# A hybrid mixer layer with 32 experts: expert weights through a ring of eight buffers, operands of the token sort stored chunk by chunk, the sort split 128 and 384

## The reference

```
h = rmsnorm(x, norm1_g)
u = h @ w_in                                   # 2048 x 5632
x = x + concat(short_conv(u_a), attention(u_q, u_k, u_v), conformer_conv(u_c)) @ w_out
h = rmsnorm(x, norm2_g)
grp = argmax(softmax(h @ rg_w + rg_b))         # 4 groups of 8 experts
e1, e2 = top 2 of softmax(h @ re_w + re_b) inside the group
for each expert e of 32, for the tokens that chose it:
    y[token] += gate * ((silu(h @ w_gate[e]) * (h @ w_up[e])) @ w_down[e])
out = rmsnorm(x + y, final_g)
```

## Time and profile before

| | us |
|---|---|
| median of 3 runs | 1378.87 (1377.28 to 1378.97) |
| the profiled execution, its own time | 1379.87 |
| its span, first to last instruction | 1378.1 |
| TensorE matmul busy | 1243.5 (90%) |
| TensorE weight load busy | 701.5 (51%) |
| VectorE busy | 508.7 (37%) |
| ScalarE busy | 276.9 (20%) |
| DMA moved | 471.69 MB, mean 342 GB/s |

### The profile page before, as it was taken

One profiled execution on the slowest core, in us unless ns is written; L12 is line 12 of the kernel. 1 busy time (PEld: TensorE's weight loads), 2 busy tenths in 40 slices (PEclk: granted clock), 3 DMA queues, 4 the chain that ended last, 5 costly groups with the idle time before them and its releaser, 6 DMA issues.

```text
span 1378.1 us, 16838 instructions
## 1 busy us (share of the span) xinstructions
PE 1243.5 (90%) x6468; PEld 701.5 (51%) x6468; DVE 508.7 (37%) x906; ACT 276.9 (20%) x383; POOL 6.0 (0%) x27
## 2 busy tenths in 40 slices
PE   5999999989989998989898989898988888988996
PEld 5999999978877433333333333333333333333332
DVE  5365968655444422222222232222222222222224
ACT  5433444445332100010000010000110000100002
POOL 1000000000000000000000000000000000000000
PEclk9999999999989999999999999999999999999998
DMA  8555454538466699999999999999999999999993
GB/s 274 196 184 184 150 185 148 169 141 296 162 244 244 259 428 428 428 430 428 428 428 429 428 428 430 428 428 431 427 428 430 428 428 430 428 427 430 429 423 148
DMA packets 63580, 471.69 MB, mean 342 GB/s; under 512 B 5911, under 2 KB 6423, under 8 KB 37692
## 3 DMA queue, kind: packets, MB, share of 16 engines
q1 hardware_dynamic: 63548, 471.24, 83.6%
HBM read 469.13 MB, written 2.10 MB: 342 GB/s over the span
## 4 chain that ended last, share of the span: by engine, by line
PE 50%; DMA 45%; DVE 2%; issue 2%; SPq 1%; ACT 1%; DVEq 0%; ACTq 0%
DMA ring<-in_w_up 44%; PE bank L1275 23%; PE bank L1442 17%; PE bank L1419 2%; PE bank L1491 2%; PE bank L1443 1%; PE bank L1504 1%; SPq L384 1%; DMA stage<-in_w_in 1%; PE bank L1385 1%; DVE x_tok L1148 0%; ACT w_hi L341 0%; DVE zone_u L833 0%; PE bank L1352 0%; DVE x_tok L1236 0%
## 5 line engine op out<-in xcount | busy, mean ns | idle before, releaser
L1442 PE MATMUL bank<-ring,win 128*64 128x512 f32 x976 | 431.9, 595 | 75.7 <-DMA ring<-in_w_up 75.7
L1443 PE MATMUL bank<-ring,win 128*64 128x512 f32 x992 | 440.5, 597 | 0.0
L1442 PEld LDWEIGHTS bank<-ring,win 128*64 128x64 f32 x976 | 129.2, 137 | 346.7 <-issue 346.7
L1148 DVE TENSOR_TENSOR x_tok<-x_tok,bank 128x512 f32<-128x512 f32 x256 | 158.7, 683 | 268.8 <-PE bank L1504 267.9
L1491 PE MATMUL bank<-ring,hiddenT 128*64 128x512 f32 x1024 | 226.8, 594 | 18.2 <-issue 17.5
L347 DVE TENSOR_TENSOR w_lo<-stage,w_hi 128x2048 fp32r<-128x2048 f32 x60 | 137.6, 2300 | 94.0 <-ACT w_hi L341 93.7
L1275 PE MATMUL bank<-h_hi,w_hi 128*128 128x256 f32 x576 | 163.6, 284 | 1.5 <-DVE w_lo L347 1.5
L1275 PE MATMUL bank<-h_lo,w_hi 128*128 128x256 f32 x576 | 163.3, 283 | 0.0
L1275 PE MATMUL bank<-h_hi,w_lo 128*128 128x256 f32 x576 | 163.2, 283 | 0.0
L1491 PEld LDWEIGHTS bank<-ring,hiddenT 128*64 128x64 f32 x1024 | 84.6, 137 | 136.6 <-issue 115.8
L341 ACT ACTIVATE w_hi<-stage 128x2048 fp32r<-128x2048 f32 x60 | 114.8, 1916 | 143.7 <-PE bank L1275 140.0
(11 more groups left out here) (224 smaller groups left out, 864.5 us busy)
## 6 DMA issues: line engine op xcount, KB each, us to landing
ring<-in_w_down SPq DMA_DIRECT2D x62, 2048.0 KB, 19.9
ring<-in_w_gate SPq DMA_DIRECT2D x61, 2048.0 KB, 17.1
ring<-in_w_up SPq DMA_DIRECT2D x61, 2048.0 KB, 21.6
stage<-in_w_in SPq DMA_DIRECT2D x44, 1024.0 KB, 5.1
stage<-in_w_out SPq DMA_DIRECT2D x16, 1024.0 KB, 5.1
ring<-in_w_up SPq DMA_DIRECT2D x6, 1024.0 KB, 7.2
ring<-in_w_gate SPq DMA_DIRECT2D x4, 1024.0 KB, 13.6
ring<-in_w_down SPq DMA_DIRECT2D x4, 1024.0 KB, 20.5
```

The lines of the kernel that those rows point to most:

```text
L1148: V.tensor_tensor(at, at, bank[banks[n]][:, :], ALU.add).then_inc(returned, 1)
L1442: M.matmul(bank[0][0:W_ROWS, :], rows_of[:, c, 0:W_ROWS], gate[:, at], start=(c == 0), stop=(c == C - 1))
L1443: ins = M.matmul(bank[0][UPPER, :], rows_of[:, c, 0:W_ROWS], up[:, at], start=(c == 0), stop=(c == C - 1))
```

## The change

- **Layout.** `h2_hi` and `h2_lo` are written chunk by chunk: `"p (t c k) -> p t c k"`. Every chunk's 128 weights are now neighbours for TensorE. The two passes that write them (ACT L676, DVE L1063; now L703 and L1087) read x_tok with the step of 16 floats instead.
- **Split.** SORT = 128. The first part sorts slots 0 to 127, with the same 64 matmuls of 128 columns; the second part slots 128 to 511, 64 matmuls of 384 columns, one chunk to a bank over seven banks, so that a matmul group waits for the eviction of the chunk seven before it. The transposition of `hidden` now waits for the last eviction.
- **Ring.** Eight buffers. Piece n = 6e + k goes to a slot that turns with n modulo 8; it waits for the use of piece n - 8. `ring[0]` to `ring[6]` take the first seven pieces, as before; `ring[7]` lies where h2 lies and is free only when the second part of the sort is done. The loop runs over rounds of four experts (24 pieces, three turns of the ring). The crowded-expert path, behind a flag, has its own semaphores.

```diff
+RING = 8
+LATE = 7
+LATE_FROM = 4
+ROUND = 4
-SORT = SLOTS // 2
+SORT = P
...
-        ring = [sb(f"ring{k}", [P, PIECE]) for k in range(PIECES)]
-        ahead = sb("ahead", [P, PIECE])
+        ring = [sb(f"ring{k}", [P, PIECE]) for k in range(RING - 1)]
...
+        ring.append(sb("ring7", [P, PIECE]))
-        h2_hi_c, h2_lo_c = (z[:, :].rearrange("p (t k c) -> p t c k", t=T, c=C) for z in (y_hi, y_lo))
+        h2_hi_c, h2_lo_c = (z[:, :].rearrange("p (t c k) -> p t c k", t=T, c=C) for z in (y_hi, y_lo))
+        x_tok_c = x_tok[:, :, :].rearrange("p t (k c) -> p t c k", c=C)
...
+        def piece_at(e, k):
+
+            n = PIECES * e + k
+            if n < RING - 1:
+                return n, 16
+            turn, at = divmod(n - (RING - 1), RING)
+            slot = at if at < LATE_FROM else LATE if at == LATE_FROM else at - 1
+            return slot, 16 * (turn + 1 + (slot != LATE) + (slot < 2))
...
+                for k, part in ((up_first, HALF[h]), (gate_last, HALF[h])):
+                    sp.wait_ge(in_used, h + 1)
+                    slot = slot_of(1, k)
+                    sp.dma_start(ring[slot][:, part], second[k][:, part]).then_inc(piece_loaded[slot], 16)
...
+            def load_next(e, k, slot, src):
+
+                lead = k - RING
+                wait_used(e + lead // PIECES, lead % PIECES)
+                load_piece(slot, src[k])
+
+            sp.wait_ge(in_used, QUARTERS)
+            load_piece(slot_of(1, up_last), second[up_last])
+            load_piece(slot_of(1, down_first), second[down_first])
+            sp.wait_ge(sorted2_done, C)
+            load_piece(slot_of(1, down_last), second[down_last])
+            third = expert_pieces(2)
+            sp.wait_ge(down_used, 2)
+            load_piece(slot_of(2, gate_first), third[gate_first])
+            sp.wait_ge(down_used, J)
+            load_piece(slot_of(2, up_first), third[up_first])
+            sp.wait_ge(in_used, QUARTERS + 2)
+            load_piece(slot_of(2, gate_last), third[gate_last])
+            for k in (up_last, down_first, down_last):
+                load_next(2, k, slot_of(2, k), third)
...
-                nc.scalar.activation(h2_hi[:, t, :], x_tok[:, t, :], ACT.Copy, scale=RSTD[:, t:t + 1]).then_inc(h2_hi_made, 1)
+                nc.scalar.activation(h2_hi_c[:, t], x_tok_c[:, t], ACT.Copy, scale=RSTD[:, t:t + 1]).then_inc(h2_hi_made, 1)
...
-                V.scalar_tensor_tensor(h2_lo[:, t, :], x_tok[:, t, :], RSTD[:, t:t + 1], h2_hi[:, t, :].bitcast(F32),
+                V.scalar_tensor_tensor(h2_lo_c[:, t], x_tok_c[:, t], RSTD[:, t:t + 1], h2_hi_c[:, t].bitcast(F32),
                                        ALU.mult, ALU.subtract).then_inc(h2_lo_made, 1)
```

More of the change, by code:

```diff
@@ L405, in _ @@
             gate_first, up_first, gate_last, up_last, down_first, down_last = range(PIECES)
-            pieces = [expert_pieces(e) for e in range(3)]
-            sp.dma_start(ahead[:, :], pieces[1][gate_first]).then_inc(ahead_loaded, 16)
+            second = expert_pieces(1)
+            load_piece(slot_of(1, gate_first), second[gate_first])
             for h in range(2):
-                sp.wait_ge(in_used, h + 1)
-                sp.dma_start(ring[1][:, HALF[h]], pieces[1][up_first][:, HALF[h]]).then_inc(up1_loaded[h], 16)
-                sp.dma_start(ring[0][:, HALF[h]], pieces[2][gate_first][:, HALF[h]]).then_inc(gate2_loaded[h], 16)
@@ L413, in load_second @@
-            def load_second(t, src):
-                sp.wait_ge(in_used, QUARTERS * t)
-                load_piece(gate_last, src[gate_last])
-                load_piece(up_last, src[up_last])
-            def load_down(t, src):
-                sp.wait_ge(down_used, J * t + (J // 2 - J))
-                load_piece(down_first, src[down_first])
-                sp.wait_ge(down_used, J * t)
-                load_piece(down_last, src[down_last])
-            def load_first(t, src):
-                sp.wait_ge(in_used, QUARTERS * t + (2 - QUARTERS))
-                load_piece(gate_first, src[gate_first])
-                load_piece(up_first, src[up_first])
@@ L450, in _ @@
-            with sp.Fori(3, E - 1) as e:
-                load_expert(e, e)
+            with sp.Fori(1, E // ROUND - 1) as i:
+                for r in range(ROUND):
+                    e = i * ROUND + r
+                    src = expert_pieces(e)
+                    for k in range(PIECES):
+                        load_next(e, k, slot_of(ROUND + r, k), src)
+            for e in range(E - ROUND, E - 1):
+                src = expert_pieces(e)
+                for k in range(PIECES):
+                    load_next(e, k, slot_of(e, k), src)
@@ L1528, in _, with expert @@
                 ins.then_inc(sorted2_done, 1)
-            pe.wait_ge(sorted2_act, 2)
+            pe.wait_ge(sorted2_dve, 10 // 2 + 1)
             turn_gates(0)
+            pe.wait_ge(sorted2_act, 15 // 2 + 1)
             turn_hidden(0)
-            pe.wait_ge(sorted2_dve, 3)
-            down(0, down_arrived(0))
-            def expert(t, waits, gate, up, arrived):
+            down(0, piece(0, 4), piece(0, 5), arrived_down(0))
+            def expert(t, of, waits, arrived):
                 pe.wait_ge(win_ready, t)
@@ L1576, in steady @@
-            def steady(t):
-                def waits(q):
-                    if q == 0:
-                        for k in (0, 1):
-                            pe.wait_ge(piece_loaded[k], 16 * t - 16)
-                    if q == 2:
-                        second_half(t)
-                return waits
-            def last_waits(q):
-                if q == 0:
-                    for k in (0, 1):
-                        pe.wait_ge(piece_loaded[k], 16 * (E - 1) - 16)
+                down(t, piece(of, 4), piece(of, 5), arrived)
@@ L1603, in _ @@
-            expert(2, waits2, ring[0], ring[1], down_arrived(2))
+            for e in range(1, ROUND):
+                expert(e, e, arrived_in(e), arrived_down(e))
             pe.wait_ge(tables_ready, 1)
             flag = pe.value_load(over_i[0:1, OVER:OVER + 1], min_val=0, max_val=E)
-            with pe.Fori(3, E - 1) as e:
-                expert(e, steady(e), ring[0], ring[1], down_arrived(e))
-            expert(E - 1, last_waits, ring[0], ring[1], last_arrived)
+            assert ROUND * PIECES % RING == 0
@@ L1610, in _ @@
+            per_round = 16 * ROUND * PIECES // RING
+            with pe.Fori(1, E // ROUND - 1) as i:
+                for r in range(ROUND):
+                    of, more = ROUND + r, i * per_round - per_round
+                    expert(i * ROUND + r, of, arrived_in(of, more), arrived_down(of, more))
+            for e in range(E - ROUND, E - 1):
+                expert(e, e, arrived_in(e), arrived_down(e))
+            expert(E - 1, E - 1, last_in_arrived, last_arrived)
             banks_free(E - 1, 0)
```

167 lines of the change are left out of this document (75 added, 92 removed).

## The result

| | before | after |
|---|---|---|
| median of the runs, us | 1378.88 (1377.28 to 1378.97, 4 runs) | 1369.66 (1366.95 to 1370.21, 4 runs) |
| ratio | | 0.9932, 95% interval 0.9915 to 0.9949 |
| span of the profiled execution | 1378.1 | 1368.4 |

The change gains 9.2 us, not 16.1. The direction was right; the time lies above the range. In the changed kernel the sort is L1445, `gate_up` L1468 and L1469, `turn_gates` L1478, `turn_hidden` L1485, `down` L1503, and SP loads pieces at L398 and L426.

A forecast was written before the change was run, and what follows sets the result against it. The expert-weight stream was taken as the bound, so only its idle time ahead of 475 us counted. Part 2's 11.5 plus Part 1's 4.6 made 16.1 us, forecasting 1362.8 us, range 1358.0 to 1368.5.

The forecast's parts named there:

- The tail: From the last expert's first product to the span's end: 44.8 us, left as it was.
- Part 1: First part of the sort: 112 ns per matmul, low passes waiting for h2_lo, expert 0 starting at 417.3 instead of 421.9; gains 4.6 us.
- The layout's other cost: DVE's passes writing h2_lo now read x_tok with a 64-byte step: 3.6 us each instead of 2.3; ACT's extra time hidden.
- The rival of 4.6: Strided passes cost more: a DVE pass takes 4.6 us, expert 0 starts at 419.3, gain 14.1, 1364.8 us; chance 0.17.
- the one of free strides: Strided passes on DVE cost nothing extra: expert 0 starts at 414.7, gain 18.7, 1360.2 us; chance 0.13.
- Part 2: Weight stream from expert 0's start (x): the fifteenth piece starts at x + 41.7 instead of x + 53.2; gains 11.5 us.
- missed its gap: Rival: the eighth buffer's or an old `ahead` piece meets an overlooked wait, 4.9 us of gap stay, 1367.7 us; chance 0.07.
- coin toss inside the forecast: Slower matmuls, seen in the last expert, may also hit expert 0's first products: 1.6 us slower.
- Nothing given back in the 852 us: The stretch of the 174 pieces behind the saturated stream's start keeps its length: 0 us lost.
- The step was not the cause: Rival: sort matmuls stay at 224 to 228 ns whatever layout and columns; 8.3 us gain remain, 1370.6 us; chance 0.07.
- The slower long queue: Rival: up to six open pieces instead of four lower the transfer rate; at 414 GB/s 1391.6 us; chance 0.04.
- The term of 1.6 us: Last expert: slow matmuls (1.06 us where others take 0.6) for about 3 us cost some 1.6 us and may not recur.

The follow-up runs named there:

- the even split: The changed kernel with its sort split 256 and 256 again, new layout and eight-buffer ring kept: 1361.27 us, ratio 0.9885.
- the last kernel: Changed kernel with 256/256 sort, only experts 0, 1, 2 and the last written out, and three unused matmuls ahead of the sort: 1359.52 us.
- the warm kernel: The changed kernel with three matmuls, their result overwritten, put in TensorE's idle time before the sort: 1367.53 us, ratio 0.9927.
- no ring: The changed kernel with the six buffers, `ahead` and loads of the kernel before; new layout and 128/384 split kept: 1375.70 us, ratio 0.9981.
- old layout: The changed kernel with the old layout of h2 (64-byte step on TensorE), 128/384 split and ring kept: 1373.00 us, ratio 0.9967.
- thirds: The changed kernel with the second part's 64 matmuls of 384 columns cut into 192 of 128: 1379.17 us, ratio 1.0006.
- the short code: The changed kernel with 256/256 sort and a longer TensorE loop, only experts 0, 1, 2 and the last written out: 1359.74 us, ratio 0.9861.

## Why the prediction missed

- **The bound** was read rightly. The time of every kernel here follows the moment from which the stream never stops. With the ring and the even split that is already expert 0's first quarter, and the fifteenth piece waits in the queue. The tail was left at 44.8 and measured 44.75, and that was luck: both traces have a stretch at the half clock in the last expert that eleven of the other twelve lack, with a tail of 43.1.
- **Part 1** is the step that failed. "With adjacent weights and 128 columns I take 112 ns, the row of 40 columns": that row ran at the whole clock, and the sort starts at the half one. The rows read for the prediction did not show it, as the windows of the earlier trace rows begin at 409, though their mean of 0.88 over 409 to 426 said that the first part had not run at the whole clock throughout; the trace of the kernel before has both stretches:

```profile
404.00:409.00 5.00, 2.03 (x15) 1.95 (x16) 4.64 (x30) 2.92 (x7) 0.00 (x0) 0.50 0.99 426
400.50:402.50 2.00, 1.95 (x16) 1.83 (x16) 0.71 (x4) 1.54 (x2) 0.00 (x0) 1.00 0.98 418
```

The layout alone does not change that. What stood there was 0.215 us, for all 64 matmuls, since with 128 columns the clock did not return before they ended. So x was 421.17 instead of 417.3: 3.9 of the 6.4 us missing in the trace. The old layout had hidden this: its weight load costs 0.22 to 0.23 at either clock, so the row of 228 ns did not show that its first part was run at both.
- **The layout's other cost** held: ACT's two passes took 7.41 us and DVE's 7.36, so 3.7 each, forecast 3.6. The rival of 4.6 did not occur, nor did the one of free strides. The Trainium skill's lower figure (Vector Engine (DVE) Microarchitecture Reference, 5.2 Measured stream behaviour on trn2), 1.73 ns per element for one source hopping at every element, nearly agrees: 3.7 us for 2048 elements are 1.8 ns. Its 2.50 at a step of 24 words was not reached at this step of 16 words. None of it decided the time of the change, as TensorE's low passes were later than h2_lo; in the last kernel it does, with waits of 0.68 and 1.49 us for y_lo.
- **Part 2** held in its mechanism. The second part took 11.2 us (174 ns forecast, 175 measured), down_last went out at its end, the wait for the last eviction was 0.54, and no piece missed its gap. It gained 10.5 instead of 11.5. The missing 1.0 is the half clock in expert 0's first products: its in products took 15.0 us (421.17 to 436.19) instead of 13.9. The prediction had named this and priced it at 1.6, but as a coin toss inside the forecast, where it followed from the same cause as Part 1.
- **"Nothing given back in the 852 us"** was wrong by 1.5 us, some 1.3 of them behind 1263 with the experts that are written out. The prediction counted the round of four as a few register instructions on SP and did not count TensorE's longer program. The rest, 0.2 to 0.3, lies between the fifteenth piece and 617 and was not traced.
- **The rivals.** "The step was not the cause" gave nearly the right time, 1370.6, for a wrong reason: the layout alone gains 9.6 us. The slower long queue did not show: 428 GB/s as before, though pieces now land 27 to 31 us after their issue instead of 17 to 22.

Sum in the trace: 16.1 less 3.9, less 1.0, less 1.5 is 9.7, the difference of the spans.

## What to carry to other kernels

A duration taken from one row for another place is good only at the same granted clock: look at the clock in the window where the edit will land, and for small matmuls at the weight load as well, since with adjacent weights it doubled here when the clock was halved (0.112 and 0.215). Ask of a smaller first part what sets its end; here the same 64 weight loads ran whether they carried 128 or 256 columns, so the uneven split took nothing off the first part and put 3.4 us on the second. Where a transfer stream is the bound, look also at iterations written out ahead of the end: in the traces three experts went with 0.2 to 1.5 us.

## What the hardware did that I had not expected

- A load of 128 adjacent float32r weights costs 0.112 us at the whole clock (192 in 21.5 us) and 0.215 at the half (0.226 in the low passes of the warm kernel). With a step of 64 bytes it costs 0.22 to 0.23 at either.
- With 64 matmuls of 128 columns the granted clock stayed at 0.50 through the first part and 2 to 5 us into expert 0, in four kernels (the change, no ring, old layout, thirds); with 256 columns it was back between 412 and 415, 5 to 6 us behind the sort's start. Started at 1.00, it fell to 0.50 within 4 us with 128 columns and stayed whole with 256. But 192 of the 128-column kind behind full-size products ran at 1.00 throughout.
- The same clock decides the tail. In three of the fourteen traces (the change, the kernel before and the short code) the last expert's first products met a half-clock stretch, and 44.8 us lay between its first product and the end (1315.57 to 1360.4 in the short code). In the eleven others it was absent, and the tail was 43.1 us (1315.79 to 1358.9 in the even split, 1314.54 to 1357.6 in the last kernel). The term of 1.6 us in the prediction's range is real; what brings it on stays open.
